# Reordering the attention rounds of a hybrid decoder kernel: a GpSimd wait dropped, transposes, norm steps and fillings moved

## The reference

```python
z = h @ w_in                                   # layer 0: one projection
qa, ka, va, qb, kb, vb, rb, gl = split(z)      # A: 8 heads of 64; B: 4 heads of 128
oa = dilated_attention(rope(qa), rope(ka), va) # softmax attention at dilations 1, 4 and 16
g = (gl @ w_gate_up + b_gate_up)               # rank-16 gate, decay of B
ob = rms_norm(gla(qb, kb, vb, log_sigmoid(g) / 16)) * silu(rb)
h = h + concat(oa, ob) @ w_out
h = h + conv_ffn(rms_norm(h))                  # in both layers: up, width-3 conv, silu gate, down
h = h + mixer_c(rms_norm(h))                   # layer 1: gMLP, position mixing in blocks of 128
```

## Time and profile before

| what | value |
|---|---|
| three runs | 2089.84, 2091.09, 2091.24 us; median 2091.09 |
| the profiled execution, its own time | 2089.45 us |
| its span, first to last instruction | 2087.6 us |
| PE, DVE, ACT, POOL busy | 99%, 70%, 44%, 42% of the span |
| granted TensorE clock | 0.998 of full |

### The profile page before, as it was taken

One profiled execution on the slowest core, in us unless ns is written; L12 is line 12 of the kernel. 1 busy time (PEld: TensorE's weight loads), 2 busy tenths in 40 slices (PEclk: granted clock), 3 DMA queues, 4 the chain that ended last, 5 costly groups with the idle time before them and its releaser, 6 DMA issues.

```text
span 2087.6 us, 26260 instructions
## 1 busy us (share of the span) xinstructions
PE 2062.1 (99%) x10166; PEld 1699.6 (81%) x10166; DVE 1467.3 (70%) x1728; ACT 916.9 (44%) x1274; POOL 873.3 (42%) x455
## 2 busy tenths in 40 slices
PE   8999999999999999999999999999999999999997
PEld 6888788878888888888888888888888888888886
DVE  6669775655976676677989504538877667677988
ACT  4231566744544444444435330225544444444444
POOL 3332112232787777760002332444877776820000
PEclk9999999999999999999999999999999999999999
DMA  4111001032222221228983111113321221249872
GB/s 169 41 31 41 21 31 32 31 122 91 81 91 91 91 81 71 91 72 306 389 298 114 51 51 31 51 41 121 111 89 63 91 91 68 84 140 384 302 282 81
DMA packets 95165, 235.95 MB, mean 113 GB/s; under 512 B 10113, under 2 KB 12482, under 8 KB 95042
## 3 DMA queue, kind: packets, MB, share of 16 engines
q1 hardware_dynamic: 93170, 229.54, 30.8%
q10 hardware_dynamic: 1872, 4.74, 0.6%
HBM read 198.59 MB, written 35.65 MB: 112 GB/s over the span
## 4 chain that ended last, share of the span: by engine, by line
PE 93%; DVE 3%; DMA 1%; SPq 1%; issue 1%; ACT 1%; POOL 0%; DVEq 0%; ACTq 0%
PE ps L1419 13%; PE ps L1420 13%; PE ps L1421 13%; PE ps L926 6%; PE ps L929 6%; PE ps L932 6%; PE ps L1453 6%; PE ps L1455 6%; PE ps L1456 6%; PE ps L1133 2%; PE ps L1135 2%; PE ps L1134 2%; PE ps L1524 1%; PE ps L1525 1%; PE ps L1526 1%; PE ps L1282 1%
## 5 line engine op out<-in xcount | busy, mean ns | idle before, releaser
L630 POOL TENSOR_TENSOR w_hi<-w_raw,ones 128x1024 fp32r<-128x1024 f32 x53 | 105.2, 1986 | 694.3 <-PE ps L932 230.2
L1419 PE MATMUL ps<-t_hi,w_hi 128*128 128x512 f32 x672 | 263.7, 392 | 0.3
L1420 PE MATMUL ps<-t_lo,w_hi 128*128 128x512 f32 x672 | 261.8, 390 | 0.0
L1421 PE MATMUL ps<-t_hi,w_lo 128*128 128x512 f32 x672 | 261.6, 389 | 0.0
L1453 PE MATMUL ps<-d_hi 128*128 128x512 f32 (+1 forms) x632 | 242.4, 384 | 0.2 <-DVE d_lo L2226 0.2
L1456 PE MATMUL ps<-d_hi,d_lo 128*128 128x512 f32 (+1 forms) x632 | 241.6, 382 | 0.0
L1455 PE MATMUL ps<-d_lo,d_hi 128*128 128x512 f32 (+1 forms) x632 | 241.6, 382 | 0.0
L690 POOL TENSOR_TENSOR w_lo<-w_sum,w_hi 128x1024 fp32r<-128x1024 f32 x84 | 231.9, 2771 | 23.2 <-ACT w_hi L2758 23.2
L690 POOL TENSOR_TENSOR w_lo<-w_raw,w_hi 128x1024 fp32r<-128x1024 f32 x84 | 157.5, 1875 | 171.0 <-ACT w_hi L2758 157.2
L1419 PE MATMUL ps<-act_hi,w_hi 128*128 128x512 f32 x504 | 196.1, 389 | 0.0
L1420 PE MATMUL ps<-act_lo,w_hi 128*128 128x512 f32 x504 | 196.1, 389 | 0.0
(11 more groups left out here) (348 smaller groups left out, 4540.4 us busy)
## 6 DMA issues: line engine op xcount, KB each, us to landing
w_raw<-w_up SPq DMA_DIRECT2D x44, 1024.0 KB, 4.8
d_ring<-w_dn SPq DMA_DIRECT2D x146, 256.0 KB, 7.9
d_ring<-g_kept SPq DMA_DIRECT2D x124, 256.0 KB, 9.6
g_kept<-gst SPq DMA_DIRECT2D x44, 512.0 KB, 2.6
w_raw<-w_in SPq DMA_DIRECT2D x24, 512.0 KB, 3.5
chain_a<-g_kept SPq DMA_DIRECT2D x44, 256.0 KB, 9.3
x_kept<-x SPq DMA_DIRECT2D x16, 512.0 KB, 9.2
x<-x_kept SPq DMA_DIRECT2D x16, 512.0 KB, 10.2
```

The lines of the kernel that those rows point to most:

```text
L1419: pe.matmul(out, wh, bh, start=(fresh and j == 0), stop=False, skip_group_check=True)
L1420: pe.matmul(out, wh, bl, start=False, stop=False, skip_group_check=True)
L1421: ins = pe.matmul(out, wl, bh, start=False, stop=(j == 3), skip_group_check=True)
```

## The change

- GpSimd: the low part of the second block of pair 1 no longer waits for A.rope 20. Of the output projection's block 3 the high part is made when its block is loaded and the scores of step 23 are done, and only the low part waits for `values` of step 27.
- `v_moves_of`: in pair 0 the moves i = 2, 3 go from steps 3, 4 to steps 4, 5. In double steps with s < 6, `v_transposes` now comes before `transposes`; on ScalarE `take_vn` comes before `take`.
- VectorE, pair 0: the wait for GpSimd goes; the ropes of Q0 move ahead of the last norm steps, and norm steps 3, 4 of head 1 move behind the maxima of steps 4, 5.
- Last pair: `fill(24)` comes before `scores(25)`; on ScalarE `spread` of chunks 1 to 3 comes one step earlier, behind `take`.
- Start: `low_rank(0)` stands behind k = 2 instead of k = 0.

```diff
@@ gpsimd
             low_part((N_A + 3) % 2, (N_A + 3) % 2, N_A + 5)
-            pool.wait_ge(A.rope, 20)
             low_part((N_A + 4) % 2, (N_A + 4) % 2, N_A + 6)
...
-            plain(N_WO + 3, 3, (A.pv, STEPS_A - 4))
+            n = N_WO + 3
+            pool.wait_ge(s_wdma[n % 2], 16 * (n // 2 + 1))
+            pool.wait_ge(A.s, 2 * DOUBLE)
+            pool.tensor_tensor(w_hi[:, 3, :], w_raw[:, n % 2, :], ones[:, 0:1].to_broadcast([P, 1024]), ALU.mult
+                               ).then_inc(s_whi, 1)
+            pool.wait_ge(A.pv, STEPS_A - 4)
+            low_part(n % 2, 3, n + 2)
@@ v_moves_of
-            return {3: ((0, 2),), 4: ((0, 3),)}.get(s, ())
+            return {4: ((0, 2),), 5: ((0, 3),)}.get(s, ())
@@ tensor
-                if k == 0 or k == 4:
+                if k == 2 or k == 4:
                     low_rank(k // 4)
...
+                    moves = v_moves_of(g + i)
+                    if s < SA - 2:
+                        for target, m in moves:
+                            v_transposes(target, m)
+                        moves = ()
                     transposes(g + i, 0)
                     transposes(g + i, 1)
-                    moves = v_moves_of(g + i)
...
+                if g == DOUBLE:
+                    fill(g)
                 if g + 1 < STEPS_A:
                     scores(g + 1)
-                fill(g)
+                if g > DOUBLE:
+                    fill(g)
@@ vector
                         take_part(0, Q1, (1, 2))
-                        dve.wait_ge(s_wsplit, N_A + 5)
-                        out_step(1, 0, 0)
-                        out_step(1, 0, 1)
+                        for step_n in range(2):
+                            out_step(1, 0, step_n)
...
                         take_part(1, K0, (1, 2))
-                        for step_n in range(2):
+                        take_part(1, Q0, (0,))
+                        out_step(1, 1, 0)
+                    elif s == 3:
+                        for step_n in range(1, 3):
                             out_step(1, 1, step_n)
-                    elif s == 3:
-                        take_part(1, Q0, (0,))
-                        for step_n in range(2, 5):
+                        dve.wait_ge(B.o[1], 8)
+                        take_part(1, Q0, (1, 2))
+                    elif s == 4:
+                        for step_n in range(3, 5):
                             out_step(1, 1, step_n)
-                    elif s == 4:
-                        take_part(1, Q0, (1, 2))
@@ scalar
+                moves_taken(g)
                 take(g, 0)
                 take(g, 1)
-                moves_taken(g)
...
+                if s == 4:
+                    moves_taken(g + 1)
                 take(g + 1, 0)
                 take(g + 1, 1)
-                moves_taken(g + 1)
+                if s != 4:
+                    moves_taken(g + 1)
...
-                if 1 <= s < 5:
-                    spread(hp - 1, s - 1)
+                if s == 1:
+                    spread(hp - 1, 0)
...
                 if hp == NHP - 1:
+                    if 1 <= s < 4:
+                        spread(hp - 1, s)
```

More of the change, by code:

```diff
@@ L478, in build @@
         STEPS_A = SA * NHP
+        DOUBLE = SA * (NHP - 1)
         R_A = 6 * NBP
@@ L835, in score_stat @@
             return a_class[:, hp % 2, s - NEAR, i:i + 1]
-        DOUBLE = SA * (NHP - 1)
         def scores_bank(g, h):
```

## The result

The changed kernel takes 2096.6 us (median of 17 executions, 2094.59 to 2099.58) where the kernel before takes 2091.24 us (17 executions, 2088.74 to 2094.46). The ratio is 1.0025, with a 95% interval of 1.0018 to 1.0033: slower by 0.25%, 5.4 us. The profiled execution is one of the longer ones, 2099.16 us, with a span of 2097.4 us.

The account below looks back on a forecast made before the run. TensorE, busy 99% of the span, was taken as the bound. Start -0.1, pair 0 +0.5, pairs 1 and 2 -0.5, last pair +3.7 make +3.6 on 2091.09: 2094.7 us, range 2086 to 2097.

Parts of the forecast that it names:

- The side: Whole kernel: slower by more than 0.2%, above 2095.3 us, chance 0.33.
- a rival that was given 0.08: Two stalls of 3.4 to 4 us let TensorE's clock fall, costing 2.5 us more: 2097.2 us, chance 0.08.
- The turns of GpSimd and VectorE: GpSimd splits and VectorE's SBUF steps block each other for a whole instruction; VectorE gains only 0.3 us in pair 0.
- Pair 0: GpSimd's wait goes, but K1 is taken no earlier and four transposes follow the stall: +0.5 us.
- The signs: Expected in the changed trace for pair 0: no wait for w_lo, one for a_sh of 3 us or more.
- Pairs 1 and 2: Class transposes ahead of transposes(8) and (16) remove both waits for a_vc: -0.5 us, bounds -0.9 and 0.
- The filling: Last pair: filling before scores(25) delays V0's taking; a wait of 1.4 us is traded for one of 2.6.
- Block 3: Last pair: early high part blocks attention_low; take_out(27) 4.2 us later, stalling values(28); the 0.79 us a_far wait goes.
- The start: First low_rank behind k = 2 shrinks and fills the gap before it: -0.1 us; bounds 0.3 gained, 1.7 lost.
- The other rivals: Last-pair turns fall otherwise, 2091.3 us, chance 0.2; waits go and nothing comes back, 2085.3 us, chance 0.17.
- the rival with only the filling hurting: Only the filling hurts, the rest about as forecast: 2091.5 to 2093.5 us; chance counted within the forecast's 0.55.

Follow-up runs that it names:

- experiment 5: Kernel before with pair 0's edits alone (GpSimd's and VectorE's waits dropped, class transposes and norm steps reordered): 2091.5 us, 1.0000.
- experiment 11: Kernel before with only the filling of step 24 moved ahead of scores(25): 2095.65 us, 1.0016.
- experiment 1: Changed kernel with the filling of step 24 put back behind scores(25): 2092.65 us, 1.0005.
- experiment 10: Kernel before with only the high part of the output projection's block 3 made early: 2093.65 us, 1.0009.
- experiment 2: Changed kernel with both parts of block 3's split back behind values(27): 2095.16 us, 1.0021.
- experiment 7: Kernel before with only low_rank(0) moved behind k = 2: 2090.26 us, 0.9997.
- experiment 6: Kernel before with only the class transposes of pairs 1 and 2 ahead of the transposes, and ScalarE's copies ahead: 2089.21 us, 0.9991.
- experiment 3: Changed kernel with VectorE taking V0 of the last pair before the maxima of step 25: 2091.95 us, 1.0009.
- experiment 4: Changed kernel plus eleven unread matmuls in front of the V0 transposes of step 24: 2094.7 us, 1.0018.
- experiment 9: Changed kernel plus unread matmuls (12, 11 and 9) in its three long TensorE waits: 2092.85 us, 1.0005.
- experiment 12: Changed kernel with low-rank products and block 3 as before, last-pair V0 and pair 0's K1 taken earlier, pair 0's two dropped waits restored: 2088.0 us, 0.9986.

## Why the prediction came out as it did

The time, 2096.6 us, lies in the range, 1.9 us above the forecast. The side was given 0.33: the forecast itself sat inside 0.2%, and the result is outside it. The mechanisms were mostly right, and the sum was made up wrongly: the reordering by itself costs 2 to 3 us where 3.6 were forecast, and a rival that was given 0.08 made about half of the loss or somewhat more. That the forecast came within 1.9 us is in part luck.

**The turns of GpSimd and VectorE.** Right. After, in pair 0 (POOL, then DVE):

```profile
233.33 2.90 POOL L637 TENSOR_TENSOR w_lo<-w_raw,w_hi 128x1024 fp32r<-128x1024 f32 x1 [5.59 <-ACT w_hi L2624]
...
233.30 0.68 DVE L1877 TENSOR_TENSOR a_sh<-a_sh,ropeS 128x512 f32<-128x512 f32 x1
234.08 2.70 DVE L1885 TENSOR_TENSOR a_qsum<-a_sh 128x512 f32<-128x512 f32 x1
237.98 1.22 DVE L1786 SCALAR_TENSOR_TENSOR b_st<-b_st,b_e 128x1024 f32<-128x1024 f32 x1
```

GpSimd's 2.90 us hold 0.5 in which the rope step of 233.30 had its turn. The next rope step, 0.69 us in the earlier trace rows, takes 2.70 while the low part runs, and VectorE reaches the norm steps at 237.98 us where it was 238.06. As everything there begins 0.48 us later than before, that is a gain of 0.56 us where 0.3 was forecast, and far from the 2.48 us that VectorE no longer idles. The Trainium skill (SBUF — State Buffer, section "SBUF: two separate sides") calls the shared port pair an exclusive lock. These rows agree with it. One reading in the forecast's account of the turns is off by a tenth: from 259.50 to 261.77 us are 2.27, not 2.37; nothing hangs on it.

**Pair 0.** The signs came as listed: no wait for w_lo, and one for a_sh at 268.5 us, of 2.78 us where "3 us or more" was said. From 22 us to `values(4)` the profiles differ by +1.6 us, of which 1.7 are the clock, so -0.1 us against the +0.5 forecast; alone the edits measure 0.0 us, with 1.9 us to either side (experiment 5). A wait of 0.8 us for ScalarE's a_s is new there, since ScalarE takes the class copies first. It stands at 264.9 us, ahead of the longer wait for a_sh, and so costs nothing; the forecast had looked for it behind that wait.

**Pairs 1 and 2.** Both waits for a_vc went. The forecast was -0.5 us; the profile has -1.1 (from +2.11 to +0.99), and alone the part measures -2.0, with an interval that reaches zero. The term was set too small: it counted only the waits, and the profile is outside its bound of -0.9.

**The filling.** The chain was right: V0 is taken at 406.32 us, 3.60 behind the start of the maxima (3.33 before), and TensorE waits 2.74 us where 2.6 were forecast. DVE and PE after:

```profile
402.72 0.42 DVE L1905 CUSTOM_DVE_ANT_0 a_s<-ps,lmul 128x256 f32<-128x256 f32 x1 [2.66 <-PE ps L1230]
405.28 1.04 DVE L1856 TENSOR_TENSOR a_vt<-ps,rstd 128x512 f32<-128x512 f32 x1 [0.27 <-issue]
406.38 1.12 PE L1155 MATMUL ps<-cst,a_vt 128*128 128x128 f32 x4 [2.74 <-DVE a_vt L1856]
```

This is the term that was mis-sized. "A wait of 1.4 is traded for one of 2.6" counted 1.4 us (its own times give 1.2 to 1.3). The waits alone are 1.0 to 1.3 us (experiments 11 and 1), the whole is 3.95 undone and 4.5 alone; in the profile `scores(24)` to `scores(30)` lose 4.0 us, of which 3.2 are the clock. The four transposes behind the wait take 1.12 us, not the 0.60 of the earlier trace rows: the clock is already down.

**Block 3.** The blocking was forecast well: the two `attention_low` take 6.21 us where 6.6 were forecast (424.1 to 430.7). POOL, DVE and PE after:

```profile
427.41 2.39 POOL L637 TENSOR_TENSOR w_lo<-w_raw,w_hi 128x1024 fp32r<-128x1024 f32 x1
429.75 2.35 POOL L676 TENSOR_TENSOR w_hi<-w_raw,ones 128x1024 fp32r<-128x1024 f32 x1
432.24 3.16 POOL L637 TENSOR_TENSOR w_lo<-w_raw,w_hi 128x1024 fp32r<-128x1024 f32 x1
...
430.27 6.21 DVE L1980 TENSOR_TENSOR act_lo<-oT,act_hi 128x1024 fp32r<-128x1024 f32 x2
436.41 0.41 DVE L1963 COPY oT<-ps 128x256 f32<-128x256 f32 x1
...
433.24 0.80 PE L1192 MATMUL ps<-act_hi,w_hi 128*128 128x512 f32 x1 [2.12 <-DVE act_lo L1980]
```

Where TensorE meets it was wrong. The wait was placed before `values(28)`, at line 1282, with 3 to 4 us. The forecast took `take_out(27)` for what TensorE meets first and passed over the pieces of the output projection that read act_lo, ahead of `values(28)`. The wait stands before these, with 2.1 us, and before `values(28)`, at 437.05 us, there is none: `take_out(27)` is done by 436.82. (Alone, in experiment 10, both waits are there, 1.0 and 1.4 us.) Without the filling's 1.4 us the forecast for this part is +2.3 us: alone it loses 2.05 us in the profile and 2.5 in the median (experiment 10), beside the filling 1.4 (experiment 2). That term was about right.

**The start.** +0.48 us in the profile against -0.1 forecast, outside its bound of +0.3, by when the clock rose in that execution, and nothing measurable alone (experiment 7).

**The clock.** The rival had the mechanism ("a long stall lets the clock fall") and nearly the size, 2.5 us. Its chance was far too low, for a poor reason: the profile of before shows the clock at full speed behind a wait of 1.64 us, and I took that one execution for the rule. It isn't even the rule there: in experiments 6, 7 and 10 the clock fell behind the same wait. Experiments 1 and 3 give back more (3.95 and 4.65 us) than the waits that they remove, and experiments 4 and 9 give back 1.9 and 3.75 us although they shorten nothing that another engine does and add work to TensorE. Experiment 9 is the cleanest, as no other engine's order is touched.

The granted clocks of the single executions give the size a second time. The mean of (1 - c) x span is 8.5 us over the 17 executions of the changed kernel and 4.9, 5.5 and 5.2 us over the three groups of the kernel before, most of it in every kernel at the very end, where the profile of before has 0.50 from 2080.7 us on with no matmul left to slow down. The difference is what counts. The mean times are 2096.8 and 2091.3 us. So of 5.5 us at most 3.3 are the clock, at most because a low stretch costs nothing where it lies in a wait, and at least 2.2 are the reordering. From the other side, experiment 9 is 1.7 us over the kernel before, and its mean of (1 - c) x span is 3.8 us where that kernel has 5.2, so that the reordering costs up to 3.1 us. All this is an estimate, as each clock is rounded to a thousandth and the stretch at the end differs by a microsecond or two: 2 to 3 us are the reordering, and some 2.5 to 3.3 us the clock.

The Trainium skill (TensorE: Matmul & The Clock Gate, section "What's actually happening") says that idleness takes the clock to 1.2 GHz. The traces agree on the level, with 0.52 granted behind the wait of 2.74 us, but idleness alone doesn't decide it: the clock stayed at 1.00 behind waits of 2.4 and 2.8 us, and at 1198 us it fell with TensorE busy.

The other rivals fall. GpSimd and VectorE took turns in the last pair as forecast (6.21 us, and 6.24 in experiment 10), and the waits that went came back in other places. Of the rival with only the filling hurting this much holds: alone the filling loses more than any other part does alone, and mostly by way of the clock.

**Open.** What decides in which execution the clock falls isn't settled: waits of 2.4 and 2.8 us passed without (experiments 11 and 2), one of 1.6 us didn't (experiments 6, 7 and 10). Nor is it known why the clock was low at 1198 us. That the 2.0 us of experiment 6 are more than its waits is as little explained.

## What to carry to other kernels

Before moving independent work ahead to fill a wait, name the later wait that it filled until now, and move the producer of that one first: the same filling cost 4.5 us with V0 taken late, and with V0 taken early it left no wait of more than 0.2 us around it (experiment 3). A wait of two or three microseconds on a TensorE that is otherwise full has two prices, itself and the clock behind it, and the second may be the larger (2.74 and about 3.2 us at the V0 transposes). Several short waits seem better than one long one of the same sum: no profile has a fall of the clock behind a single wait of 1.4 us or less, but no experiment tested it by itself. GpSimd's work on SBUF belongs beside VectorE's steps that read PSUM, not beside those that read and write SBUF: `take_out(27)` keeps its 0.41 us beside the split of 425.39 us, while a rope step of 0.69 us takes 2.70.

## What the runs showed of the hardware

The granted clock fell to half behind waits of only 1.6 to 2.8 us, each time for 3 to 4 us and once for nearly 7 (in the changed kernel 0.50 from 269.40 to 272.80 and from 405.95 to 412.70 us). It fell shortly before TensorE resumed (at the V0 transposes of the changed kernel), as it resumed, or up to about 2 us later (experiment 4, where TensorE resumes at 431.63 us and the clock is 0.50 from 433.8 us on). Over all profiles:

| wait of TensorE | the clock fell | it stayed at 1.00 |
|---|---|---|
| a_sh, 2.8 us | changed kernel, 1, 2, 3, 4, 5 | in none |
| a_vt, 2.4 to 2.8 us | changed kernel (2.7) | 2 (2.8), 11 (2.4) |
| act_lo, 2.1 us | changed kernel, 1; 3 and 4, there with a wait of 1.4 us for oT behind it | in none |
| a_sh, 1.6 us | 6, 7, 10 | before, 11 |
| single waits of 1.4 us or less | in none | in all |

Behind the wait of 1.6 us, the windows of experiments 7 and 10:

```profile
266.60:269.90 3.30, 3.27 (x8) 2.59 (x9) 2.91 (x6) 0.33 (x1) 0.00 (x0) 0.50 0.00 0
268.60:271.90 3.30, 3.30 (x8) 2.65 (x9) 2.91 (x6) 0.23 (x1) 0.00 (x0) 0.50 0.00 0
```

The same kernel does it in one execution and not in the next, in steps that show in the times: three executions at about 2091 us and nine at about 2096 (experiment 11). The clock is not the whole spread between executions: those of experiment 12, whose waits in the rounds are all under 1.3 us and whose mean clocks are all 0.997 or 0.998, still differ by 4.7 us, and the time at which the clock rises at the start moves a matmul behind it by 2.6 us. Matmuls whose result nobody reads held the clock up, and a kernel with 32 of them more was 3.75 us faster.
